# Two-layer hybrid encoder with expert layer on one core: expert weights loaded in half units, twenty slots in place of ten

## The chip, the cores and the metric

The kernel runs on one core of one Trainium2 chip. The time is that of the device, in microseconds (us), from launch to end; the span is from the first to the last instruction in the profile of one execution. Smaller is better.

## The reference

Two layers over 256 tokens of width 1024, all in float32. Each layer has a mixing part (pooling and neighbourhood attention between two projections) and a channel part: a dense SwiGLU in layer 0, and in layer 1 eight expert SwiGLUs of which each token takes two. The last part is what the change touches:

```python
logits = jnp.einsum('td,de->te', xt, w_router)
top_logit, top_idx = lax.top_k(logits, TOP_K)          # TOP_K = 2 of 8 experts
gates = jax.nn.softmax(top_logit, axis=-1)
...
def run_block(args):                                   # tokens of one expert
    tok, gate, e = args
    xb = xt[tok]
    a = xb @ w_gate[e]                                 # 1024 x 3584
    b = xb @ w_up[e]                                   # 1024 x 3584
    y = (jax.nn.silu(a) * b) @ w_down[e]               # 3584 x 1024
    return y * gate[:, None]
```

Each expert has three matrices of 14.7 MB, 352 MB in all, and each is read once.

## The kernel before

The expert layer is done item by item, items 0 to 7, one expert each in the order of their token counts. An item has room for 96 tokens (three groups of 32) or 64 (two groups): `ITEM_CAP` is 96, 64, 96, 96, 64, 96, 96, 64. If counts are larger, a loop at the end runs extra items; these inputs need none.

The weights of an item come as 24 *units* of 3,584 columns by 128 partitions (1,792 KB), into ten slots of SBUF used in a ring: 8 for the gate matrix (one row tile of 128 rows each), 8 for up, and 8 for down, which is laid out so that a partition holds 28 rows of 1,024 in a run, in two halves of 14 rows, and a unit is 3.5 of these rows. `load_unit` on SyncE issues one transfer for a unit and raises `unit_landed[slot]`. Its loop waits before each issue until TensorE has raised `unit_done` for the unit that held the slot. The first ten units are loaded ahead, each as soon as the buffers under its slot are free: mixing buffers of layer 1 lie there.

TensorE runs `expert_item`. For gate and up it takes one unit after the other (`landed` waits for it), and for each of two halves (1,792 columns) and each group s calls `project_tokens`: four matmuls of 32 columns of tokens by 448 columns of weights, which run side by side in the four quarters of the array. `unit_done` rises once a unit, behind both halves. The last unit of each part also raises `gate_done` and `up_done` half by half, and ScalarE (Silu, L1141) and VectorE (product L1454, transpose L1459) turn the banks into `e`, whose `e_ready` the down part waits for. The down part goes through pairs of units: rows 0 to 2 of seven for all groups, then a wait for the second unit, row 3, and rows 4 to 6. After rows 0 to 2 of the second half come `combine` of the item before and `turn_picks`, and after row 3 `gather` for the next item.

The instruction streams are unrolled for items 0 to 7. SyncE's queue carries the unit loads alone in this phase, up to the two output transfers.

Of the kernel before, what the change touches and what calls it, by code (L numbers as in the profile page):

```python
# [12 lines left out]
P = 128  # L13
D = 1024
DT = D // P
# [17 lines left out]
FE = 3584  # L33
# [8 lines left out]
FH = FE // 2  # L42
FJ = FH // 4
DJ = D // 4
FT = FH // P
# [9 lines left out]
DENSE_LOADS = 3 * DBLOCKS  # L55
MOE0 = 2 * MIX_LOADS + DENSE_LOADS
assert 2 * MOE0 % STAGE == 0
UNIT = FE
SLOTS = 10
EXTRA_SLOTS = 8  # L60


def ffn_order(blocks):
# [6 lines left out]

DENSE = ffn_order(DBLOCKS)

UNITS = 3 * DT
EXTRA_TURNS = UNITS // EXTRA_SLOTS
HALF_UNITS = DT // 2
BANKS = 2 * TG
PARTS = BANKS - 1
assert UNITS % EXTRA_SLOTS == 0 and HALF_UNITS * UNIT == FT * D
# [20 lines left out]
def hybrid_encoder(nc, x, mix_pre, mix_post, ffn_pre, ffn_post, w_in, pool_w, pool_scale, rpb,  # L99
                   w_out, d_gate, d_up, d_down, router, e_gate, e_up, e_down, consts, out):  # L100
    with ExitStack() as ctx:
# [76 lines left out]
        e = hid[:, :, :, :].rearrange("p h s (t r) -> p h s t r", r=Q)  # L178
# [175 lines left out]
        MH = 2 * MOE0  # L354

        def quad(j):
            return slice(Q * j, Q * (j + 1))
# [4 lines left out]
        def ready_count(i, half, s, groups):  # L362
            return i * BANKS + (half * TG + (TG if s == groups - 1 else s + 1))
# [10 lines left out]
        def unit_slot(i, u):  # L374
            return (i * UNITS + u) % SLOTS if isinstance(i, int) else u % EXTRA_SLOTS

# [19 lines left out]
        def _(sp):  # L396
# [31 lines left out]
                            load(MIX_LOADS + j, by_tile(w[0])[:, :, cut], DT)  # L428

            def load_unit(i, expert, u):  # L430
                part, v = u // DT, u % DT
                if part == 2:
                    src = e_down[0, expert].rearrange("e (h p t) n -> p (e h) (t n)", h=2, p=P)
                    at = v % HALF_UNITS * UNIT
                    src = src[:, v // HALF_UNITS, at:at + UNIT]
                else:
                    src = (e_gate, e_up)[part][0, expert].rearrange("e (t p) n -> p (e t) n", p=P)[:, v, :]
                slot = unit_slot(i, u)
                sp.dma_start(units[slot][:, :], src).then_inc(unit_landed[slot], 16)

            zeroth = slice(0, 1)
            sp.wait_ge(scored, GROUPS * DEPTH)
            load_unit(0, zeroth, 0)
            sp.wait_ge(delta_dve_ready, DEPTH)
            load_unit(0, zeroth, 1)
            sp.wait_ge(pv_done, GROUPS * DEPTH)
            sp.wait_ge(delta_ready, 3 * DEPTH)
            for u in range(2, 5):
                sp.wait_ge(split_ready, 2 * (MOE0 - 4 + u))
                load_unit(0, zeroth, u)  # L450
            for u in range(5, 9):
                sp.wait_ge(half_done, MH - max(7 - u, 0))
                load_unit(0, zeroth, u)
            sp.wait_ge(rms_post, 2 * 3)
            load_unit(0, zeroth, 9)
            for u in range(SLOTS, UNITS):
                sp.wait_ge(unit_done, u - SLOTS + 1)
                load_unit(0, zeroth, u)
# [192 lines left out]
        def _(pe):  # L651
# [253 lines left out]
            def expert_item(i, groups, before, after, first=False, last=False, extra=False):  # L905

                def landed(u):
                    pe.wait_ge(unit_landed[unit_slot(i, u)], unit_loads(i, u) * 16)

                def project_tokens(dt, u, half, s):  # L910
                    w = units[unit_slot(i, u)]
                    for j in range(4):
                        at = half * FH + j * FJ
                        ins = mm(bank(half, s)[quad(j)], xT[:, s, dt, :], w[:, at:at + FJ],  # L914
                                 start=dt == 0, stop=dt == DT - 1)
                    return ins

                def project_hidden(half, u, tiles, s):
                    for t in tiles:
                        for j in range(4):  # L920
                            at = t * D + j * DJ
                            w = units[unit_slot(i, u + at // UNIT)][:, at % UNIT:at % UNIT + DJ]
                            ins = mm(down_out[s][quad(j)], e[:, half, s, t, :], w, start=half == t == 0 and s != 2,  # L923
                                     stop=half == 1 and t == FT - 1, skip_group_check=s == 2)
                    return ins

                pe.wait_ge(x_ready, i + 1)
                if not first:
                    pe.wait_ge(facc_done, ends(i) if extra else i)
                for dt in range(DT):  # L930
                    landed(dt)
                    for half in range(2):
                        for s in range(groups):
                            ins = project_tokens(dt, dt, half, s)
                            if dt == DT - 1 and (half, s) != (1, groups - 1):
                                ins.then_inc(gate_done, count_step(half, s, groups))
                    ins.then_inc(unit_done, 1)
                for dt in range(DT):
                    u = DT + dt
                    landed(u)  # L940
                    for half in range(2):
                        for s in range(groups):
                            if dt == 0:
                                pe.wait_ge(silu_done, ready_count(i, half, s, groups))
                            ins = project_tokens(dt, u, half, s)
                            if dt == DT - 1 and (half, s) != (1, groups - 1):
                                ins.then_inc(up_done, count_step(half, s, groups))
                    ins.then_inc(unit_done, 1)
                if not first:
                    pe.wait_ge(y_act, i)  # L950
                for v in range(0, DT, 2):
                    half, u = v // HALF_UNITS, 2 * DT + v
                    h0 = 2 * DT + half * HALF_UNITS
                    row = 7 * (v % HALF_UNITS) // 2
                    landed(u)
                    for s in range(groups):
                        if v % HALF_UNITS == 0:
                            pe.wait_ge(e_ready, ready_count(i, half, s, groups))
                        project_hidden(half, h0, range(row, row + 3), s)
                    if v == HALF_UNITS:  # L960
                        if not (first or extra):
                            combine(i - 1, before)
                        turn_picks(i, groups)
                    landed(u + 1)
                    for s in range(groups):
                        ins = project_hidden(half, h0, range(row + 3, row + 4), s)
                    ins.then_inc(unit_done, 1)
                    if v == HALF_UNITS:
                        pe.wait_ge(spread_ready, i + 1)
                        gather(i + 1, after)  # L970
                    for s in range(groups):
                        ins = project_hidden(half, h0, range(row + 4, row + 7), s)
                    ins.then_inc(unit_done, 1)
                if last or extra:
                    combine_end(i, groups)

# [20 lines left out]
        def _(act):  # L997
# [136 lines left out]
            def expert_item(i, groups, first=False, extra=False):  # L1134
                for half in range(2):
                    for s in range(groups):
                        if (half, s) == (1, groups - 1):
                            act.wait_ge(unit_done, i * UNITS + DT)
                        else:
                            act.wait_ge(gate_done, i * PARTS + bank_count(half, s, groups))  # L1140
                        act.activation(hid[:, half, s, :], bank(half, s), ACT.Silu).then_inc(  # L1141
                            silu_done, bank_step(s, groups))
                act.wait_ge(spread_tp, i + 1)
                if not first:
                    act.wait_ge(comb_done, ends(i) - 1 if extra else i)
                act.activation(spread[:, :, 0:groups, :], pa[:, :].rearrange("p (t s n) -> p t s n", t=NT, n=P)[  # L1146
                    :, :, 0:groups, :], ACT.Copy).then_inc(spread_ready, 1)
                act.wait_ge(unit_done, i * UNITS + UNITS)
                both = pd[:, :].rearrange("p (b n) -> p b n", b=2)[:, :, 0:DJ]
                ins = act.activation(y[:, 0:2, :], both, ACT.Copy)  # L1150
                if groups == TG:
                    ins = act.activation(y[:, 2, :], down_out[2], ACT.Copy)
                ins.then_inc(y_act, 1)
# [28 lines left out]
        def _(dve):  # L1182
# [259 lines left out]
            def hidden(i, half, s, groups):  # L1442
# [5 lines left out]
                if order >= 2:  # L1448
                    dve.wait_ge(e_ready, ready_count(i, (order - 2) // groups, (order - 2) % groups, groups))
                if (half, s) == (1, groups - 1):  # L1450
                    dve.wait_ge(unit_done, i * UNITS + 2 * DT)
                else:
                    dve.wait_ge(up_done, i * PARTS + bank_count(half, s, groups))
                dve.tensor_tensor(buf.rearrange("p t r -> p r t"),  # L1454
# [100 lines left out]
```

## Time and profile before

| | |
|---|---|
| median of 3 runs | 1385.05 us (1382.86 to 1386.51) |
| the profiled execution | 1383.68 us |
| its span | 1381.9 us |
| granted TensorE clock, mean | 0.981 of full speed |
| TensorE busy | 1293.9 us, 94% |
| ScalarE, VectorE busy | 278.1 and 421.2 us |
| bytes moved | 443.42 MB, mean 321 GB/s |
| expert phase, from TensorE's first matmul on a unit | 547.5 us to the end |

The span has the two mixing parts and the dense part in its first 540 us, and the expert phase behind. Engines are named as PE (TensorE matmuls), PEld (TensorE weight loads), DVE (VectorE), ACT (ScalarE), POOL (GpSimd) and SPq (SyncE's queue of DMA issues). The time of a busy TensorE is modelled from issue times, so it can read full where it is merely fed in order. The TensorE clock has two levels, 2.4 GHz (1.00) and 1.2 GHz (0.50).

### The profile page before, as it was taken

What the parts mean: (1) busy time and instruction counts of PE and PEld (TensorE: products, weight loads), DVE (VectorE), ACT (ScalarE), POOL (GpSimd) and SP (SyncE); (2) the same over time, 40 slices, a digit from 0 to 9 for tenths busy, and PEclk for the clock granted to TensorE, in tenths of its full rate; (3) what the DMA queues carried; (4) which work ended last, traced back from release to release, by engine and by line L of the source; (5) the groups of instructions that cost most, each with busy time, mean ns of one, the idle gap of its engine ahead of it and who ended that gap; (6) DMA issues with size and microseconds to landing.
All of it is one profiled execution on the core that took longest, in us unless ns stands there. A gap on an engine that the chain in (4) does not pass through costs nothing.

```text
span 1381.9 us, 30957 instructions
## 1 busy us (share of the span) xinstructions
PE 1293.9 (94%) x14359; PEld 803.1 (58%) x14359; DVE 421.2 (30%) x573; ACT 278.1 (20%) x409; POOL 103.7 (8%) x239
## 2 busy tenths in 40 slices
PE   5788999999989886999999999999989999999985
PEld 5776999999978874336344345346334345336333
DVE  5586644444455754011020031030021031031023
ACT  4355444433343533000000000000000000000001
POOL 3231400000000123700000000000000000000000
PEclk9999999999998999999999999999999999999998
DMA  9716755555554057999999999999999999999992
GB/s 312 241 62 215 218 186 185 188 188 187 186 195 148 34 228 320 379 406 389 408 426 424 426 424 424 426 425 425 425 425 426 425 427 422 428 423 424 421 416 97
DMA packets 63734, 443.42 MB, mean 321 GB/s; under 512 B 4440, under 2 KB 6496, under 8 KB 39024
## 3 DMA queue, kind: packets, MB, share of 16 engines
q1 hardware_dynamic: 61456, 433.46, 77.4%
q0 software_dynamic: 2144, 7.90, 2.0%
q8 instruction: 117, 1.92, 0.6%
q14 instruction: 17, 0.14, 0.0%
HBM read 440.30 MB, written 1.05 MB: 319 GB/s over the span
## 4 chain that ended last, share of the span: by engine, by line
PE 83%; DMA 7%; DVE 5%; ACT 1%; SPq 1%; issue 1%; POOL 0%; ACTq 0%; DVEq 0%
PE pd L923 17%; PE pa L914 13%; PE pb L914 13%; PE pc L914 9%; DMA unit<-in_moe_w_down 5%; PE pc L656 3%; PE pc L657 3%; PE pc L658 3%; PE pd L658 2%; PE pd L657 2%; PE pd L656 2%; DMA rwords_b<-in_na_rpb 2%; PE pa L656 2%; PE pa L658 2%; PE pa L657 2%; PE pa L868 2%
## 5 line engine op out<-in xcount | busy, mean ns | idle before, releaser
L923 PE MATMUL pd<-unit,hid 128*32 128x256 f32 x4704 | 260.2, 379 | 9.8 <-DMA unit<-in_moe_w_down 9.8
L914 PE MATMUL pa<-unit,xT 128*32 128x448 f32 x2048 | 240.2, 541 | 3.3 <-DMA unit<-in_moe_w_up 2.1
L914 PE MATMUL pb<-unit,xT 128*32 128x448 f32 x2048 | 240.3, 541 | 0.0
L923 PEld LDWEIGHTS pd<-unit,hid 128*32 128x32 f32 x4704 | 151.2, 110 | 116.4 <-DMA unit<-in_moe_w_down 11.9
L1196 DVE TENSOR_TENSOR w_lo<-ring,w_hi 128x2048 fp32r<-128x2048 f32 x72 | 170.7, 2372 | 139.6 <-ACT w_hi L1012 139.2
L1454 DVE TENSOR_TENSOR hidp<-hid,pa 128x448 f32<-128x448 f32 x16 | 14.8, 924 | 558.4 <-PE pa L914 558.4
L1012 ACT ACTIVATE w_hi<-ring 128x2048 fp32r<-128x2048 f32 x72 | 137.3, 1908 | 69.9 <-PE pb L658 56.4
L914 PE MATMUL pc<-unit,xT 128*32 128x448 f32 x1280 | 149.5, 539 | 0.0
L914 PEld LDWEIGHTS pa<-unit,xT 128*32 128x32 f32 x2048 | 66.3, 110 | 128.1 <-issue 120.4
L914 PEld LDWEIGHTS pb<-unit,xT 128*32 128x32 f32 x2048 | 66.6, 110 | 126.6 <-issue 126.6
L656 PE MATMUL pc<-hT_hi,w_hi 128*128 128x256 f32 x448 | 130.1, 290 | 5.4 <-DVE w_lo L1196 4.0
L657 PE MATMUL pc<-hT_lo,w_hi 128*128 128x256 f32 x448 | 128.7, 287 | 0.0
L658 PE MATMUL pc<-hT_hi,w_lo 128*128 128x256 f32 x448 | 128.5, 287 | 0.0
L1146 ACT ACTIVATE spread<-pa 128x768 f32<-128x768 f32 (+1 forms) x8 | 5.9, 733 | 441.5 <-PE pa L901 441.5
L656 PEld LDWEIGHTS pc<-hT_hi,w_hi 128*128 128x128 f32 x448 | 88.2, 197 | 6.2 <-DVE w_lo L1196 4.1
L657 PEld LDWEIGHTS pc<-hT_lo,w_hi 128*128 128x128 f32 x448 | 88.2, 197 | 0.0
L658 PEld LDWEIGHTS pc<-hT_hi,w_lo 128*128 128x128 f32 x448 | 88.0, 196 | 0.0
L914 PEld LDWEIGHTS pc<-unit,xT 128*32 128x32 f32 x1280 | 41.5, 110 | 78.8 <-issue 78.8
L658 PE MATMUL pd<-hT_hi,w_lo 128*128 128x256 f32 x256 | 72.4, 283 | 0.0
L657 PE MATMUL pd<-hT_lo,w_hi 128*128 128x256 f32 x256 | 72.4, 283 | 0.0
L656 PE MATMUL pd<-hT_hi,w_hi 128*128 128x256 f32 x256 | 72.4, 283 | 0.0
L1141 ACT ACTIVATE hid<-pa 128x448 f32<-128x448 f32 x16 | 8.7, 545 | 229.8 <-PE pa L914 229.3
(261 smaller groups left out, 1321.9 us busy)
## 6 DMA issues: line engine op xcount, KB each, us to landing
unit<-in_moe_w_gate SPq DMA_DIRECT2D x64, 1792.0 KB, 27.7
unit<-in_moe_w_up SPq DMA_DIRECT2D x64, 1792.0 KB, 26.9
unit<-in_moe_w_down SPq DMA_DIRECT2D x64, 1792.0 KB, 28.8
ring<-in_dense_w_gate SPq DMA_DIRECT2D x8, 2048.0 KB, 8.9
ring<-in_dense_w_up SPq DMA_DIRECT2D x8, 2048.0 KB, 8.9
ring<-in_dense_w_down SPq DMA_DIRECT2D x8, 2048.0 KB, 7.6
ring<-in_w_in SPq DMA_DIRECT2D x7, 2048.0 KB, 7.9
ring<-in_w_out SPq DMA_DIRECT2D x4, 2048.0 KB, 11.7
```

Source lines behind the costliest of these rows:

```text
L656: mm(dst, still[0], moving[0], start=start, stop=False)
L657: mm(dst, still[0], moving[1], start=False, stop=False)
L658: return mm(dst, still[1], moving[0], start=False, stop=stop)
L868: ins = mm(gather_out[s][quad(j)], pick[:, t, Q * s:Q * (s + 1)], blocks, start=t == 0, stop=t == NT - 1)
L914: ins = mm(bank(half, s)[quad(j)], xT[:, s, dt, :], w[:, at:at + FJ], start=dt == 0, stop=dt == DT - 1)
L923: ins = mm(down_out[s][quad(j)], e[:, half, s, t, :], w, start=half == t == 0 and s != 2, stop=half == 1 and t == FT - 1, skip_group_check ...
L1012: act.activation(hi, src, ACT.Copy).then_inc(hi_ready, 1)
L1141: act.activation(hid[:, half, s, :], bank(half, s), ACT.Silu).then_inc(silu_done, bank_step(s, groups))
L1146: act.activation(spread[:, :, 0:groups, :], pa[:, :].rearrange("p (t s n) -> p t s n", t=NT, n=P)[:, :, 0:groups, :], ACT.Copy).then_inc(s ...
L1196: dve.tensor_tensor(lo, src, hi.bitcast(F32), ALU.subtract).then_inc(split_ready, 1)
L1454: dve.tensor_tensor(buf.rearrange("p t r -> p r t"), hid[:, half, s, :].rearrange("p (r t) -> p r t", t=FT), bank(half, s).rearrange("p (r ...
```

## The change

A unit becomes half as wide: `UNIT = FH`, 1,792 columns of one gate or up row tile, or 1.75 rows of down weights. There are twenty slots in the same SBUF, 48 units an item, and so twice as many transfers, each of 896 KB with 7,168 bytes in a run for each partition instead of 14,336. The first ten row tiles are loaded in pairs under the waits of before (`load_row`). TensorE waits for and frees each half by itself, except the last row tile of gate and of up, whose two halves are freed together. In the down part the loop over rows is outside and the one over groups inside; a row waits for the units that begin in it, and a unit is freed behind the row in which it ends. The points of `combine`, `turn_picks` and `gather` are the same.

```diff
-UNIT = FE
-SLOTS = 10
-EXTRA_SLOTS = 8
+UNIT = FH
+SLOTS = 20
+EXTRA_SLOTS = 16
-UNITS = 3 * DT
+UNITS = 6 * DT
-HALF_UNITS = DT // 2
+HALF_UNITS = DT
             def load_unit(i, expert, u):
-                part, v = u // DT, u % DT
+                part, v = u // (2 * DT), u % (2 * DT)
...
-                    src = (e_gate, e_up)[part][0, expert].rearrange("e (t p) n -> p (e t) n", p=P)[:, v, :]
+                    src = (e_gate, e_up)[part][0, expert].rearrange("e (t p) n -> p (e t) n", p=P)
+                    src = src[:, v // 2, v % 2 * UNIT:(v % 2 + 1) * UNIT]
...
+            def load_row(k):
+                for u in range(2 * k, 2 * k + 2):
+                    load_unit(0, zeroth, u)
...
                 for dt in range(DT):
-                    landed(dt)
                     for half in range(2):
+                        u = 2 * dt + half
+                        landed(u)
                         for s in range(groups):
-                            ins = project_tokens(dt, dt, half, s)
+                            ins = project_tokens(dt, u, half, s)
...
-                    ins.then_inc(unit_done, 1)
+                        if dt < DT - 1:
+                            ins.then_inc(unit_done, 1)
+                        elif half:
+                            ins.then_inc(unit_done, 2)
...
-                for v in range(0, DT, 2):
-                    half, u = v // HALF_UNITS, 2 * DT + v
-                    h0 = 2 * DT + half * HALF_UNITS
-                    row = 7 * (v % HALF_UNITS) // 2
-                    landed(u)
-                    for s in range(groups):
-                        if v % HALF_UNITS == 0:
-                            pe.wait_ge(e_ready, ready_count(i, half, s, groups))
-                        project_hidden(half, h0, range(row, row + 3), s)
-                    if v == HALF_UNITS:
-                        if not (first or extra):
-                            combine(i - 1, before)
-                        turn_picks(i, groups)
-                    landed(u + 1)
-                    for s in range(groups):
-                        ins = project_hidden(half, h0, range(row + 3, row + 4), s)
-                    ins.then_inc(unit_done, 1)
-                    if v == HALF_UNITS:
-                        pe.wait_ge(spread_ready, i + 1)
-                        gather(i + 1, after)
-                    for s in range(groups):
-                        ins = project_hidden(half, h0, range(row + 4, row + 7), s)
-                    ins.then_inc(unit_done, 1)
+                for half in range(2):
+                    h0 = 4 * DT + half * HALF_UNITS
+                    for t in range(FT):
+                        first_unit, last_unit = t * D // UNIT, ((t + 1) * D - 1) // UNIT
+                        for u in range(first_unit, last_unit + 1):
+                            if u * UNIT >= t * D:
+                                landed(h0 + u)
+                        for s in range(groups):
+                            if t == 0:
+                                pe.wait_ge(e_ready, ready_count(i, half, s, groups))
+                            ins = project_hidden(half, h0, t, s)
+                        if (t + 1) * D % UNIT < D:
+                            ins.then_inc(unit_done, 1)
+                        if half and t == 2:
+                            if not (first or extra):
+                                combine(i - 1, before)
+                            turn_picks(i, groups)
+                        if half and t == 3:
+                            pe.wait_ge(spread_ready, i + 1)
+                            gather(i + 1, after)
```

## Rows read from the trace of the kernel before

**Rows 1.** The page: busy time of the engines, and its 40 slices.
```profile
PE 1293.9 (94%) x14359; PEld 803.1 (58%) x14359; DVE 421.2 (30%) x573; ACT 278.1 (20%) x409; POOL 103.7 (8%) x239
...
DMA  9716755555554057999999999999999999999992
```

**Rows 2.** Stretches of the expert phase: from:to, length, busy us, clock, DMA share, GB/s.
```profile
547.00:619.90 72.90, 72.39 (x772) 25.12 (x776) 4.00 (x7) 3.27 (x6) 30.80 (x143) 1.00 0.90 363
706.90:737.30 30.40, 30.40 (x554) 18.69 (x548) 8.86 (x20) 0.60 (x1) 0.00 (x0) 1.00 1.01 426
737.30:809.40 72.10, 72.10 (x772) 24.96 (x768) 3.49 (x5) 3.87 (x7) 0.00 (x0) 1.00 1.01 425
809.40:851.20 41.80, 41.80 (x766) 25.47 (x758) 10.86 (x22) 0.81 (x1) 0.00 (x0) 1.00 1.01 425
965.10:1013.00 47.90, 47.90 (x512) 16.27 (x504) 1.89 (x3) 3.05 (x6) 0.00 (x0) 1.00 1.01 426
1013.00:1032.10 19.10, 13.09 (x230) 7.18 (x227) 5.42 (x13) 0.00 (x0) 0.00 (x0) 1.00 1.00 422
1326.40:1347.10 20.70, 16.90 (x252) 8.05 (x244) 7.27 (x15) 0.00 (x0) 0.00 (x0) 0.92 0.97 411
1347.10:1365.60 18.50, 18.41 (x324) 11.41 (x324) 3.59 (x7) 0.60 (x1) 0.00 (x0) 1.00 0.30 124
```

**Rows 3.** TensorE's timeline in item 7: start, length, instructions, idle before and its releaser.
```profile
1338.55 2.80 PE L923 MATMUL pd<-unit,hid 128*32 128x256 f32 x48 [0.63 <-DMA unit<-in_moe_w_down]
1342.84 3.66 PE L923 MATMUL pd<-unit,hid 128*32 128x256 f32 x64 [1.49 <-DMA unit<-in_moe_w_down]
1347.13 2.80 PE L923 MATMUL pd<-unit,hid 128*32 128x256 f32 x48 [0.63 <-DMA unit<-in_moe_w_down]
```

**Rows 4.** DMA from 700 to 1300 us: packets by size; queue, packets, MB, share.
```profile
DMA packets 19984, 254.84 MB, mean 425 GB/s; under 512 B 2215, under 2 KB 2215, under 8 KB 2215
...
q1 hardware_dynamic: 19916, 253.77, 100.0%
```

**Rows 5.** The chain that ended last, its end: start, length, what.
```profile
1311.41 35.68 DMA unit<-in_moe_w_down
1347.13 2.80 PE pd L923 x48
...
1356.91 8.68 PE pd L923 x160
```

**Rows 6.** Timeline of TensorE and SyncE's queue around the first refill.
```profile
547.51 0.96 PE L914 MATMUL pa<-unit,xT 128*32 128x448 f32 x8 [1.25 <-DVE xT L1422]
...
549.03 0.94 PE L914 MATMUL pc<-unit,xT 128*32 128x448 f32 x8
...
552.28 22.88 SPq L439 DMA_DIRECT2D unit<-in_moe_w_up  x6
```

**Rows 7.** The unit loads (L439) issued from 552 to 560 us.
```profile
DMA to landing us min/median/max: 7.2/8.0/8.8
```

**Rows 8.** The unit loads (L439) issued from 640 to 662 us.
```profile
L439 SPq DMA_DIRECT2D unit<-in_moe_w_up x3: 332/332/333, 655.0 to 661.9; - x3
...
DMA to landing us min/median/max: 8.7/9.4/11.0
```

**Rows 9.** DMA from 153.4 to 155.4 us, packets of 2 KB: packets, MB, share.
```profile
q1 hardware_dynamic: 400, 0.82, 105.0%
```

**Rows 10.** DMA from 437.4 to 439.4 us, packets of 4 KB.
```profile
q1 hardware_dynamic: 206, 0.84, 102.4%
```

**Rows 11.** Timeline at the start of item 0's down part.
```profile
619.34 0.91 DVE L1454 TENSOR_TENSOR hidp<-hid,pc 128x448 f32<-128x448 f32 x1
619.69 2.56 PE L923 MATMUL pd<-unit,hid 128*32 128x256 f32 x44
...
620.28 0.65 DVE L1459 STREAM_TRANSPOSE hid<-hidp 128x448 f32<-128x448 f32 x1
```

**Rows 12.** DMA from 1340 to 1370 us in 40 slices of 0.75 us.
```profile
DMA  9999999664544635446444331200000000000000
GB/s 440 421 401 459 421 440 421 268 287 194 229 191 191 268 153 248 210 191 268 175 210 191 134 134 57 90 0 0 0 0 0 0 0 0 0 0 0 0 22 0
```

More of the change, by code:

```diff
@@ L441, in _ @@
             zeroth = slice(0, 1)
+            def load_row(k):
+                for u in range(2 * k, 2 * k + 2):
+                    load_unit(0, zeroth, u)
             sp.wait_ge(scored, GROUPS * DEPTH)
-            load_unit(0, zeroth, 0)
+            load_row(0)
             sp.wait_ge(delta_dve_ready, DEPTH)
-            load_unit(0, zeroth, 1)
+            load_row(1)
             sp.wait_ge(pv_done, GROUPS * DEPTH)
             sp.wait_ge(delta_ready, 3 * DEPTH)
[L448 to L453, printed above, removed]
+            for k in range(2, 5):
+                sp.wait_ge(split_ready, 2 * (MOE0 - 4 + k))
+                load_row(k)
+            for k in range(5, 9):
+                sp.wait_ge(half_done, MH - max(7 - k, 0))
+                load_row(k)
             sp.wait_ge(rms_post, 2 * 3)
-            load_unit(0, zeroth, 9)
+            load_row(9)
             for u in range(SLOTS, UNITS):
@@ L912, in project_tokens @@
                     for j in range(4):
-                        at = half * FH + j * FJ
+                        at = j * FJ
                         ins = mm(bank(half, s)[quad(j)], xT[:, s, dt, :], w[:, at:at + FJ],
@@ L916, in project_tokens, with project_hidden @@
                     return ins
[L918 to L924, printed above, removed]
+                def project_hidden(half, u, t, s):
+                    for j in range(4):
+                        at = t * D + j * DJ
+                        w = units[unit_slot(i, u + at // UNIT)][:, at % UNIT:at % UNIT + DJ]
+                        ins = mm(down_out[s][quad(j)], e[:, half, s, t, :], w, start=half == t == 0 and s != 2,
+                                 stop=half == 1 and t == FT - 1, skip_group_check=s == 2)
                     return ins
@@ L930, in expert_item @@
                 for dt in range(DT):
-                    landed(dt)
                     for half in range(2):
+                        u = 2 * dt + half
+                        landed(u)
                         for s in range(groups):
-                            ins = project_tokens(dt, dt, half, s)
+                            ins = project_tokens(dt, u, half, s)
                             if dt == DT - 1 and (half, s) != (1, groups - 1):
                                 ins.then_inc(gate_done, count_step(half, s, groups))
-                    ins.then_inc(unit_done, 1)
+                        if dt < DT - 1:
+                            ins.then_inc(unit_done, 1)
+                        elif half:
+                            ins.then_inc(unit_done, 2)
                 for dt in range(DT):
-                    u = DT + dt
-                    landed(u)
                     for half in range(2):
+                        u = 2 * DT + 2 * dt + half
+                        landed(u)
                         for s in range(groups):
@@ L947, in expert_item @@
                                 ins.then_inc(up_done, count_step(half, s, groups))
-                    ins.then_inc(unit_done, 1)
+                        if dt < DT - 1:
+                            ins.then_inc(unit_done, 1)
+                        elif half:
+                            ins.then_inc(unit_done, 2)
                 if not first:
                     pe.wait_ge(y_act, i)
-                for v in range(0, DT, 2):
-                    half, u = v // HALF_UNITS, 2 * DT + v
-                    h0 = 2 * DT + half * HALF_UNITS
-                    row = 7 * (v % HALF_UNITS) // 2
-                    landed(u)
-                    for s in range(groups):
-                        if v % HALF_UNITS == 0:
-                            pe.wait_ge(e_ready, ready_count(i, half, s, groups))
-                        project_hidden(half, h0, range(row, row + 3), s)
-                    if v == HALF_UNITS:
-                        if not (first or extra):
-                            combine(i - 1, before)
-                        turn_picks(i, groups)
-                    landed(u + 1)
-                    for s in range(groups):
-                        ins = project_hidden(half, h0, range(row + 3, row + 4), s)
-                    ins.then_inc(unit_done, 1)
-                    if v == HALF_UNITS:
-                        pe.wait_ge(spread_ready, i + 1)
-                        gather(i + 1, after)
-                    for s in range(groups):
-                        ins = project_hidden(half, h0, range(row + 4, row + 7), s)
-                    ins.then_inc(unit_done, 1)
@@ new lines, in expert_item @@
+                for half in range(2):
[10 more added lines that the diff above has]
+                        if (t + 1) * D % UNIT < D:
+                            ins.then_inc(unit_done, 1)
+                        if half and t == 2:
[5 more added lines that the diff above has]
+                            gather(i + 1, after)
@@ L1137, in expert_item @@
                         if (half, s) == (1, groups - 1):
-                            act.wait_ge(unit_done, i * UNITS + DT)
+                            act.wait_ge(unit_done, i * UNITS + 2 * DT)
                         else:
@@ L1450, in hidden @@
                 if (half, s) == (1, groups - 1):
-                    dve.wait_ge(unit_done, i * UNITS + 2 * DT)
+                    dve.wait_ge(unit_done, i * UNITS + 4 * DT)
                 else:
```

## Prediction

> **What bounds the kernel now.** I read the page first, for where the time is. In its slices the expert phase is more than half the span, and there both TensorE and the DMA engines read nine tenths or more [rows 1]. Two full engines do not say which one is late, so the second view is the stretches of the phase. An item with 96 slots costs TensorE 72.1 us for its 16 gate and up units, 4.51 us a unit, and 41.8 us for the 8 down units with combine and gather; an item with 64 slots costs 47.9 us (3.0 us a unit) and 30.4 us [rows 2]. So TensorE wants 113.9 us or 78.3 us for an item. The transfers take the same time for each. How long is in the third view, TensorE where it waits: in item 7, the last, it starts again at 1338.55, 1342.84 and 1347.13 us, each time released by a unit that landed, 4.29 us apart [rows 3]. Twenty-four units are then 103 us: DMA is faster than a long item, and 25 us slower than a short one. Over the five long and three short items TensorE wants 804 us, and transfers at 4.29 us for 192 units 824 us. From 706.9 us to 1300 us the DMA share never reads under 1.00 [rows 2, 4], while TensorE waits a few us in the last two thirds of two short items (13.09 us busy of 19.10, 16.90 of 20.70) [rows 2]. So what ends last is the queue of transfers: it never runs dry after the first item, it decides when the item 7's unit 20 (the fifth down unit) lands, and only 18.5 us of TensorE work and the final norm lie behind that [rows 2, 5]. The chain says the same: 35.68 us of transfer up to 1347.13 us, then only TensorE [rows 5]. A cost on each byte's transfer is paid in full. TensorE's own time is paid only behind the last wait.
>
> In item 0 it is otherwise. The first refill waits until TensorE has finished unit 0: issued at 552.28 us, with TensorE started at 547.51 us [rows 6]. It lands in 7.2 us [rows 7], of which 4.29 us are pace and 2.9 us latency. From there slots come free every 4.51 us, slower than 4.29 us, so the queue is shallow: at 640 to 662 us a unit still lands 8.7 us after its issue, 1.5 us more than with an empty queue [rows 8]. Behind that, short item 1 frees slots every 3.0 us and the queue stays deep to the end.
>
> **The transfers, cut in two.** Bytes, order and engines stay. A unit is now one packet of 14,336 bytes for each of 128 partitions: 8 packets on each of 16 DMA engines, and one small completion word. (17,700 large packets and 2,215 small ones in 600 us are this 8 to 1 [rows 4].) After the change it is 16 packets of 7,168 bytes and two words. No row shows a 7,168-byte packet, so I take its pace from packets of other sizes, in stretches of 2 us where nothing else moves and all engines are full. 2 KB: 400 packets, so 16 x 2 us / 400 = 80.0 ns [rows 9]. 4 KB: 206 packets, 155.3 ns [rows 10]. The line through them is 4.7 ns a packet and 0.0368 ns a byte. It gives 531.8 ns at 14,336 bytes; the measured 4,290 / 8 = 536 ns are 4.4 ns more, with the completion word in them. So the line holds over a sevenfold size. At 7,168 bytes it gives 268.3 ns. Sixteen are 4,292 ns against 8 x 531.8 = 4,254 ns: 38 ns more for two half units. The second completion word I price like any packet, 5 ns. The pace becomes 4.29 + 0.043 = 4.333 us for the bytes of one unit, 1.0% slower.
>
> Bounds: a packet constant and a word that cost nothing give 4.290 us. From above: the shares in the same rows count 105.0% and 102.4% busy, so a packet is held for 84.0 and 159.1 ns, and that line has a constant of 8.9 ns; if none of this overlapped, eight more packets and a word are 80 ns, 4.370 us. I take 4.333 us, as the packet counts are throughput and the shares are occupancy.
>
> How many units pay: the wait that decides is for the item 7's unit 20. From the first refill (unit 10 of the phase) to there are 178 units: 178 x 0.043 = +7.6 us (bounds 0 and +14.2 us).
>
> A rule of the Trainium skill bears on that constant. By "DMA: Bandwidth & Descriptors", section "Why small descriptors are slow (HBM only)", each packet pays a fixed overhead of some 3 cycles; with the 850 MHz of the same page's "Where 436 GB/s comes from" that is 3.5 ns, an estimate from the page, below the 4.7 ns of [rows 9, 10]. Eight more packets would then be 28 ns a unit and 178 units +5.0 us, where the rows give +7.6 us.
>
> **The start of the refilling.** The slot of half unit 0 comes free after 2.26 us of TensorE work instead of 4.51 us, so the first refill goes out at about 550.0 us, 2.26 us earlier. Of such a lead only what the queue holds can survive the shallow stretch, and that was 1.5 us at its thinnest [rows 8]: -1.5 us for every later landing. Together +6.1 us for the second half of the deciding unit.
>
> **The finer wait.** Before, TensorE starts rows 0 to 2 of that second down half when all of unit 20 is there, and needs 2.80 us (0.87 us a row, from 160 instructions, ten rows, in 8.68 us [rows 5]). After, row 0 starts on the first half unit, 2.17 us sooner, and rows 1 and 2 (1.74 us) remain behind the second. The combine therefore comes 6.1 - 0.9 = 5.2 us later. Nothing behind it is late again: the last half unit is wanted by row 12, which starts about 14 us behind the combine's start, and it lands three units or 13.0 us behind the second half of unit 20, so 11.3 us behind the combine's start.
>
> **Edits that cost nothing where they lie.** Twice as many issues: 0.33 us each on SyncE's queue [rows 8], 384 of them against 2.17 us of transfer each; behind them on that queue stand only the next loads and the output. Twice the landing waits on TensorE: a boundary shows no gap, since six steps of 0.75 us [rows 6] are already the 4.51 us of a unit. Down rows looped over t outside and groups inside: the same matmuls and weight loads, but groups 1 and 2 of row 0 are wanted sooner. In item 0 the down part starts at 619.69 us, group 2's row 0 would be due 0.86 us later at 620.55 us, and its transpose ends at 620.93 us [rows 11]: 0.4 us in a long item. In a short one, with group 1 wanted 0.43 us into the part and not 1.3 us, at most 0.9 us. Sum 5 x 0.4 + 3 x 0.9 = 4.7 us if it all counted; the queued transfers hide it: already at 662 us a unit lands up to 11.0 us after its issue, 3.8 us more than with an empty queue [rows 7, 8], the depth grows from there, and in items 4 and 7 TensorE waits for transfers anyway. The gate and up parts' last bank frees both half units at once, as before. The nine prefetched units land 9 x 0.04 = 0.4 us later, and the last of them isn't wanted until 588 us.
>
> **Sum:** +7.6 - 1.5 - 0.9 = +5.2 us on the profiled execution's 1383.7 us, so 1388.9 us. Its span is 1381.9 us; the 1.8 us around it stay. The runs' median is 1385.05 us, 1.4 us above the profiled one, which gives 1390.2 us, 0.37% slower. A measurement of this kernel can tell about 0.3%, or 4.2 us, from no change, and the forecast lies just beyond that.
>
> **Rivals.**
> - *The packets are cheap.* The constant is under 4 ns at this size, or the 4.4 ns above the line shrink with shorter packets. For it: it is so small that a count of 205 and not 206 in [rows 10] would move it, and a single ns decides. Against it: two sizes far below 7 KB, and the line's hit at 14 KB. With half of it, 2.4 ns for each of eight packets and the word, 178 units cost +3.8 us and the sum is +1.4 us (1386.5 us); with no cost at all it is -2.4 us (1382.7 us). Both are within 0.3%. Chance 0.33. By the Trainium skill's 3 cycles (the section above) the sum would be +5.0 - 2.4 = +2.6 us, an estimate from that page, 1387.7 us and within 0.3% too; the line from the two sizes speaks against it, by 1.2 ns.
> - *The packets are dear.* Each packet start also repeats some of the 4.4 ns, or nothing overlaps: up to +14.2 - 1.5 - 0.9 = +11.8 us, 1396.9 us. For it: the occupancy of [rows 9, 10]. Against it: occupancy isn't pace. Chance 0.12.
> - *Faster.* The wait ends with the slowest DMA engine. From about 1345 us the engines' share drops to a half and stays there for some 11 us [rows 12]: half the engines are done that much sooner. If finer transfers made the slow ones lose less (each stop would end with 7 KB in front of it and not 14 KB), at most that lag, about 11 us, would come back. It decides from a gain of 9.4 us, which turns +5.2 us into -4.2 us. Nothing shows that the lag hangs on the unit. Chance 0.05.
> - *TensorE's new waits.* The 4.7 us of transposes reach the path, because an item that waited for transfers now waits for both. In the last item that is 0.9 us on top of +5.2 us at worst; with all of it, 1394.9 us. Chance 0.04.
>
> The forecast as it stands, a constant of 4 to 6 ns, has 0.46, with a range of its own from 1389.0 to 1392.3 us (nine times 4 or 6 ns on 178 units, less 2.4 us). The range for 8 in 10 is 1384.0 to 1396.0 us: it leaves out the free packet and the dearest ones. Faster 0.05. Slower 0.46 x 0.9 (its lower edge lies within 0.3%) + 0.12 + 0.04 = 0.57. Same is the rest, 0.38.
>
> **What would show it.** DMA packets rise by 24,576 large and 3,072 small to 91,382. In a stretch of full transfers the rate falls from 425 GB/s to about 421 GB/s, and TensorE's waiting starts in the last item come in steps of 2.17 us, not 2.145 us. The first refill is issued near 550.0 us and lands in about 5.1 us. The start of the rows behind the last combine comes 5 us later. The prediction is wrong if the rate stays at 425 GB/s (cheap), falls under 419 GB/s (dear), or if the last rows of TensorE wait for something other than a unit.

## The result, and the profile after

The changed kernel takes 1388.43 us (median of 16 runs, 1385.66 to 1392.38); the kernel before, over all its runs beside it, 1382.49 us (16 runs, 1375.14 to 1386.51). The ratio is 1.006, 95% interval 1.0044 to 1.0077, so it is 0.6% slower, clear of noise. The forecast was 1390.2 us, from a base of 1385.05 us: +5.2 us, where the medians now differ by 5.9 us and the ratio makes it some 8 us. Ratios here and below leave out disturbed executions; in e2_packets that is one of seven, of 1882.95 us at a granted clock of 0.67.

The page after, its slices and its packets. The busy times and the digits look like those of [rows 1]; what differs is the rate under them and the number of packets.

```profile
PE 1295.7 (94%) x14359; PEld 798.4 (58%) x14359; DVE 419.9 (30%) x573; ACT 277.9 (20%) x409; POOL 103.0 (7%) x239
...
DMA  9616755555554068999999999999999999999993
...
DMA packets 91384, 443.44 MB, mean 320 GB/s; under 512 B 7512, under 2 KB 9568, under 8 KB 91248
```

DMA from 700 to 1300 us, against [rows 4]. The same 600 us move 249.71 MB and not 253.77 MB, though the queue is busy all the time. The mean of 418 GB/s lies under the 419 GB/s that the prediction had named as the sign of dear packets.

```profile
DMA packets 39259, 250.80 MB, mean 418 GB/s; under 512 B 4355, under 2 KB 4355, under 8 KB 39189
...
q1 hardware_dynamic: 39189, 249.71, 100.8%
```

The timeline of TensorE in item 7, ahead of the last combine, against [rows 3]. The starts after a landing are now 2.18 us apart on average (8.71 us for four from 1345.10 us on), which is 4.355 us for the bytes of a whole unit, against 4.29 us.

```profile
1345.10 1.93 PE L927 MATMUL pd<-unit,hid 128*32 128x256 f32 x32 [1.10 <-DMA unit<-in_moe_w_down]
1347.29 1.93 PE L927 MATMUL pd<-unit,hid 128*32 128x256 f32 x32 [0.26 <-DMA unit<-in_moe_w_down]
...
1353.81 1.93 PE L927 MATMUL pd<-unit,hid 128*32 128x256 f32 x32 [1.06 <-DMA unit<-in_moe_w_down]
```

The end of the chain, against [rows 5]. It still runs through a transfer of down weights until TensorE may do rows 1 and 2 of the second half; only then come the combine and the last ten rows.

```profile
1328.94 24.83 DMA unit<-in_moe_w_down
1353.81 1.93 PE pd L927 x32
...
1362.73 8.68 PE pd L927 x160
```

The first refill, against [rows 6]: TensorE's first expert matmul, then SyncE's issue 2.52 us behind it, where it had been 4.77 us. It lands in 4.8 us.

```profile
545.31 0.96 PE L919 MATMUL pa<-unit,xT 128*32 128x448 f32 x8 [1.24 <-DVE xT L1430]
```
```profile
547.83 25.13 SPq L440 DMA_DIRECT2D unit<-in_moe_w_up  x12
```

The transfers issued from 640 to 662 us, against [rows 8]: the soonest lands in 5.3 us where it was 8.7 us, the median in 7.2 us where it was 9.4 us. Each carries half the bytes, which is some 2.2 us less by itself, so this alone doesn't show an earlier queue.

```profile
DMA to landing us min/median/max: 5.3/7.2/10.2
```

**A yardstick inside the profile.** Here the first expert matmul comes at 545.31 us and before at 547.51 us, though nothing ahead of it was changed except loads that nobody waits for; in a second profile of the kernel before it comes at 541.70 us. Single executions differ by that much ahead of the expert phase. So I compare the stretch from TensorE's first expert matmul to the start of its last ten rows: 1356.73 - 547.51 = 809.2 us before and 1362.54 - 545.31 = 817.2 us after, +8.0 us.

A sharper yardstick for the pace alone lies between two like waits. In items 4 and 7, both short, TensorE waits for the fifth down unit (after the change, for its second half). Between the two waits 72 units land. The item 4 waits of before and after, from their chains, stand below; those of item 7 are at 1347.13 us [rows 5] and 1353.81 us (above).

```profile
1032.09 2.80 PE pd L923 x48
```
```profile
1033.59 1.93 PE pd L927 x32
```

That is 315.04 us before and 320.22 us after, 4.376 and 4.447 us a unit; the second profiles of both kernels (e10_before, e11_after below) give 315.00 and 320.20 us.

### The profile page after: what moved, and what is told of

Read it like the earlier page. It is cut to its first block, busy times and chain, and to the rows that moved or that the text cites. A ratio compares the mean times of both kernels' runs of the same rounds, so it can differ in the third digit from the quotient of the medians.

```text
span 1384.6 us, 31423 instructions
## 1 busy us (share of the span) xinstructions
PE 1295.7 (94%) x14359; PEld 798.4 (58%) x14359; DVE 419.9 (30%) x573; ACT 277.9 (20%) x409; POOL 103.0 (7%) x239
## 4 chain that ended last, share of the span: by engine, by line
PE 81%; DMA 7%; DVE 7%; ACT 1%; issue 1%; SPq 1%; POOL 0%; ACTq 0%; DVEq 0%
PE pd L927 16%; PE pa L919 13%; PE pb L919 12%; PE pc L919 8%; DMA unit<-in_moe_w_down 4%; PE pc L661 3%; PE pc L662 3%; PE pc L663 3%; PE pd L663 2%; PE pd L662 2%; PE pd L661 2%; DMA rwords_b<-in_na_rpb 2%; DMA unit<-in_moe_w_up 2%; PE pa L663 2%; PE pa L661 2%; PE pa L662 2%
## 5 line engine op out<-in xcount | busy, mean ns | idle before, releaser
L927 PE MATMUL pd<-unit,hid 128*32 128x256 f32 x4704 | 263.4, 380 | 12.6 <-DMA unit<-in_moe_w_down 9.5
```

## The experiments

Ratios are against runs of the kernel before on the same chip, with 95% intervals; "stretch" is the first yardstick above, "72 units" the second.

| run | packets | ratio | stretch, us | 72 units, us | MB in 700 to 1300 us |
|---|---|---|---|---|---|
| before | 14,336 B | 1 | 809.2 | 315.0 | 253.77 |
| after | 7,168 B | 1.006 (1.0044 to 1.0077) | 817.2 | 320.2 | 249.71 |
| e1_whole | 14,336 B | 0.9986 (0.9966 to 1.0006) | 810.2 | 316.8 | 253.56 |
| e2_packets | 7,168 B | 1.0061 (1.0039 to 1.0082) | 820.0 | 319.6 | 250.34 |
| e4_quarter | 3,584 and 7,168 B | 1.0167 (1.0145 to 1.0188) | 831.8 | 325.8 | 245.12 |
| e7_parity | 14,336 B, twice the transfers | 1.0015 (0.9995 to 1.0034) | 809.2 | 315.1 | 253.75 |
| e5_hybrid | 14,336 B, halves at two places | 0.9979 (0.9959 to 0.9999) | 806.7 | - | 253.64 |
| e6_big | as e5, part 28,672 B | 0.9971 (0.9954 to 0.9987) | 804.6 | - | 253.87 |

In the last two TensorE no longer shows a wait for that unit in item 7.

### Whole transfers under the new waits (e1_whole)

```diff
 (the changed kernel; landing counted once for a pair of half units)
-                    src = src[:, v // 2, v % 2 * UNIT:(v % 2 + 1) * UNIT]
+                    src = src[:, v // 2, :]
...
-                sp.dma_start(units[slot][:, :], src).then_inc(unit_landed[slot], 16)
+                sp.dma_start(pairs[pair][:, :], src).then_inc(unit_landed[pair], 16)
```

> The changed kernel with its half-unit waits, releases and row order on TensorE, but each pair of half units is again one transfer with packets of 14,336 bytes. Packet theory (the slower pace of the 7,168-byte packets is the whole loss): the pace returns to 4.29 us for a unit's bytes, the rate from 700 to 1300 us to 425 GB/s, and the time to that of the kernel before, within 2 us. Rival, TensorE's new waits in the row order reach the path: 3 to 6 us slower than before, at 425 GB/s.

Measured: median 1378.41 us of 12 runs, ratio 0.9986. The loss goes away when only the half transfers are taken back. Everything on TensorE's side (twice the releases, the row order, the earlier wish for the transposed groups) stayed in and costs nothing that the time shows. So the rival with TensorE's waits falls. Whether packets or the number of transfers cost is left to the next two. In this profile the deciding unit came 5.97 us behind the one before it (1340.23 to 1346.20 us) and not 4.29 us; without that one late landing the stretch would read 808.5 us.

### Small packets alone (e2_packets)

```diff
 (the kernel before; a slot is two chunks with 32 bytes behind each)
+            return units[slot][:, 0:parts * (n + PAD)].rearrange("p (a n) -> p a n", a=parts)[:, :, 0:n]
...
-                sp.dma_start(units[slot][:, :], src).then_inc(unit_landed[slot], 16)
...
+                src = src.rearrange("p (a n) -> p a n", a=parts)
+                sp.dma_start(chunks(slot, parts), src).then_inc(unit_landed[slot], 16)
```

The ahead-loaded unit 6 also waits for one more half of the mixing part, since the gaps move its end.

> The kernel before, with whole units, ten slots and one transfer a unit, but each slot has a gap of 32 bytes in its middle, so that a transfer consists of 7,168-byte packets. Packet theory: 8 more packets per engine and unit at 8 ns each, pace 4.36 us a unit, rate 418 to 419 GB/s, and with neither the earlier start nor the finer wait the time is 10 to 13 us above before. Rival, the number of transfers and completion words costs and not the packets: same as before within 2 us.

Measured: median 1391.78 us of 7 runs, ratio 1.0061, stretch +10.8 us. One transfer and one completion word for each unit as before, and the whole loss is there. DMA from 700 to 1300 us of this run:

```profile
DMA packets 37174, 251.40 MB, mean 419 GB/s; under 512 B 2183, under 2 KB 2183, under 8 KB 37107
...
q1 hardware_dynamic: 37107, 250.34, 100.7%
```

The 2,183 completion words are the count of before (2,215), at the rate of after. In the time, 0.61% is 8.4 us (5.4 to 11.3), a little under the 10 to 13 us expected; the stretch lies inside. The 72 units take 4.5 us more, which is 7.8 ns for each of the eight added packets.

### Twice the transfers alone (e3_transfers, e7_parity)

```diff
 (the kernel before, landing counted to 32; e3: two runs of 64 neighbouring partitions)
-                sp.dma_start(units[slot][:, :], src).then_inc(unit_landed[slot], 16)
+                for k in range(0, P, P // 2):
+                    sp.dma_start(units[slot][k:k + P // 2, :], src[k:k + P // 2]).then_inc(unit_landed[slot], 16)
 (e7: even and odd partitions)
+                for k in range(2):
+                    sp.dma_start(units[slot][k::2, :], src[k::2]).then_inc(unit_landed[slot], 16)
```

> The kernel before, but each unit comes as two transfers of 64 partitions each, with packets of 14,336 bytes: as many transfers and completion words as in the changed kernel, and no more data packets than before. Packet theory: one more completion word of 5 ns a unit, at most 1 us in all, same as before within 2 us, 424 to 425 GB/s. Rival, the number of transfers: 10 to 13 us slower, 418 GB/s.

Measured: median 2126.95 us of 6 runs, which scatter from 1906.99 to 2130.93 us. Neither theory had this. The profiled execution is one of the longest, 2130.93 us. The experiment changed two things: each transfer covered only half of the partitions, and neighbouring ones. In the profile, DMA from 1000 to 1200 us shows the engines busy all the time at half the rate:

```profile
DMA packets 3829, 43.96 MB, mean 220 GB/s; under 512 B 764, under 2 KB 764, under 8 KB 764
...
q1 hardware_dynamic: 3816, 43.76, 100.3%
```

3,816 - 764 = 3,052 large packets in 200 us on 16 engines are 1,049 ns each instead of 536 ns. So this run says nothing on the number of transfers, and I made it again with partitions that spread.

> The kernel before, but each unit comes as two transfers, one of the even and one of the odd partitions, with packets of 14,336 bytes. Packet theory: as many data packets as before and one more completion word, some 10 ns a unit, 2 us in all, 424 GB/s. Rival, the number of transfers is what costs: 10 us or more slower, 418 GB/s. If the rate falls far below 400 GB/s, as with 64 neighbouring partitions, the partitions that one transfer covers decide it, and the run says nothing on either.

Measured: median 1382.69 us, ratio 1.0015, and the rate of before with twice the completion words:

```profile
DMA packets 22194, 254.82 MB, mean 425 GB/s; under 512 B 4426, under 2 KB 4426, under 8 KB 4426
...
q1 hardware_dynamic: 22125, 253.75, 100.1%
```

The number of transfers is not the cost of 8 us. The time puts it at 2 us, with zero inside the interval and 4.7 us at its upper end (0.34%); the profile puts it at less, since the stretch is the 809.2 us of before and the 72 units take 315.1 us against 315.0 us.

### The dose (e4_quarter)

```diff
 (e2_packets with four chunks for gate and up units, two for down; the slot's gaps to match)
-                slot, parts = unit_slot(i, u), 2 if part == 2 else 2
+                slot, parts = unit_slot(i, u), 2 if part == 2 else 4
```

> As the kernel before with 7,168-byte packets in the down units, and packets of 3,584 bytes in the gate and up units (gaps of 32 bytes in a slot). If every packet start costs its 4.7 ns of the line and also repeats the 3.7 ns of stall that the changed kernel shows, 24 more packets are 202 ns a gate or up unit and 8 more are 67 ns a down unit, 157 ns on average: 178 units give 28 us more, rate near 411 GB/s. If only the 4.7 ns of the line repeat: 88 ns on average, 16 us more. If the halving costs by something else than the number of packets, 10 to 13 us as in the run with 7,168-byte packets.

Measured: median 1404.71 us, ratio 1.0167, which is 23 us (20 to 26), and stretch +22.6 us, between the 16 us and the 28 us expected and above the 10 to 13 us of the third case. It moved 245.12 MB in the 600 us:

```profile
DMA packets 58425, 246.16 MB, mean 410 GB/s; under 512 B 2134, under 2 KB 2134, under 8 KB 58359
...
q1 hardware_dynamic: 58359, 245.12, 101.3%
```

A unit is 1.835 MB, so 600 us give 4.339 us a unit before, 4.398 us in e2 and 4.492 us here. Divided by the packets that an engine does more (8 in e2; 24, 24 and 8, on average 18.7, here), that is 7.4 ns and 8.2 ns a packet; by the 72 units it is 7.8 and 8.0 ns. The price is close to constant for each packet, and it is nearer to the full 8.4 ns (4.7 ns and the 3.7 ns more) than to the 4.7 ns of the line. In the changed kernel the same reckoning gives 4.409 us: 70 ns for eight packets and one completion word. The time grew by less than 178 x 0.153 = 27 us would say. What is missing lies ahead of item 4's wait: up to there e4 is about 12 us longer, where 106 units at 0.150 us would be 16 us. That fits refills in item 0, where slots come free only every 4.51 us, hiding part of the price. But in e2 nothing is missing (+10.8 us, where 178 x 0.063 is 11.2 us), so it stays open.

### What the finer transfers give back (e5_hybrid, e8_lead, e9_tail)

```diff
 (the changed kernel; load_unit issues n half units at once)
+            if 20 <= i * UNITS + u < 68 or (i, u // 2) == (NE - 1, 5 * DT // 2):
+                return 1
...
+            return 2
```

> As the changed kernel, but with whole transfers (packets of 14,336 bytes) everywhere except the refills behind the first twenty half units up to the fifth row tile of item 1's up... that is half units 20 to 67 of the phase, and the two half units whose landing is waited for ahead of the last combine. If the earlier start is worth 1.5 us and the finer last wait 0.9 us, as the sum had it, the time is 1 to 4 us below before (-0.1 to -0.3%); the first refill is issued 2.3 us after TensorE's first unit, and the rate from 700 to 1300 us is 425 GB/s. If neither is worth anything the time is that of the run with whole transfers everywhere, within 1 us.

Measured: 1377.85 us, ratio 0.9979, stretch 806.7 us, 2.5 us under before. The direction and the size are those expected, and the interval just leaves out 1. Then each place alone, with a second profile of both kernels for the yardstick's own spread (one execution each):

> The hybrid without its finer last wait: half transfers only for half units 20 to 67. Measured inside the profile, from TensorE's first expert matmul to the start of its last ten rows (809.2 us before, 810.2 us with whole transfers everywhere, 806.7 us in the hybrid): if the earlier start is worth 1.5 to 2.3 us, 808 to 808.7 us; if the finer wait did all, 810 us.

> The hybrid without its earlier start: half transfers only for the two half units whose landing is waited for ahead of the last combine. From 810.2 us the finer wait gives 809.3 us; if it did all that the hybrid gains, 806.7 us.

> The kernel before, unchanged, to see how far the same stretch of the profile (809.2 us) repeats: if within 1 us, differences of 2 us between single profiles mean something.

> The changed kernel again, for the same: 817.2 us in its first profile, 8.0 us more than before. The packet theory wants 7 to 9 us more in this one as well.

Measured stretches: e8_lead 807.2 us, e9_tail 808.9 us, e10_before 808.2 us, e11_after 817.5 us. The yardstick repeats within 1.0 us for before and 0.3 us for after, so the changed kernel is 8.0 to 9.2 us longer in every pairing. Against e1_whole (810.2 us) the earlier start alone gives 3.0 us, more than the 1.5 to 2.3 us expected, the finer wait alone 1.3 us, both together 3.5 us. But e1_whole has the one late landing of 1.7 us just there, so it is a poor base. Parts of the stretch tell the two gains apart more sharply:

- *The start*: from TensorE's first expert matmul to item 4's wait it is 483.6 to 485.1 us in the five profiles with whole transfers in item 0 (before, e1, e7, e9, e10), and 482.5 and 482.9 us in e8 and e5. The means differ by 1.6 us, with a spread of 1.5 us. This is what is left of the gain, since in e8 and e5 the 24 units that go out as halves also have the small packets.
- *The finer wait*: from item 7's wait for the fourth down unit to the last ten rows it is 13.9 us in before, e8 and e10 and 13.1 us in e5 and e9. That is 0.8 us each time.

### Packets of 28,672 bytes (e6_big)

```diff
+            if i in (1, 2, 3, 5, 6) and u >= 4 * DT:
+                return 4
```

> As the hybrid, and the down weights of items 1, 2, 3, 5 and 6 in transfers of four half units, packets of 28,672 bytes. If the packet cost of 8.4 ns holds on to larger packets, four packets fewer for a unit's bytes and half a completion word are 36 to 40 ns, 40 units give 1.5 us back: 0 to 2 us below the hybrid. If the packet cost ends at 14 KB, the same as the hybrid or a little above it, since slots come free and units land four at a time.

Measured: 1377.99 us, ratio 0.9971, stretch 804.6 us, 2.1 us under the hybrid. The times of the two can't be told apart (0.9979 and 0.9971), the stretch leans to a packet cost that goes on at larger sizes. So does a part of it that repeats well: from item 4's wait to that for the fourth down unit of item 7 it is 310.7 to 310.8 us in five profiles with 14 KB packets (before, e10, e5, e8, e9) and 310.2 us here. Sixteen units lie in it with the larger packets, so each gives back about 30 ns, near the 36 to 40 ns expected. This version is clearly faster than the kernel before, by 0.29% (0.13 to 0.46%), and so faster than both.

## Why the prediction was right, and where a term was off

**What bounds the kernel** was right: the queue of transfers. In e2 and e4 TensorE's work is that of before, and the time follows the pace of the transfers.

**The pace of the half transfers** had the right mechanism and too small a size. It is the term that was off. I took +0.043 us for a unit's bytes. The rows after give +0.070 us by rate (4.339 to 4.409 us), +0.065 us by the starts in item 7 (4.29 to 4.355 us) and +0.072 us by the 72 units. By the prediction's own sign (a rate under 419 GB/s) the packets are dear, which I had given a chance of 0.12, though far from the dearest case of 80 ns. The step from the line to the full queue was wrong: I took the line's 4.7 ns for the whole price of a packet, and what lay above it at 14 KB for a share of time that would not repeat with more packets. The dose run shows that about 3 ns more do repeat. I had also read what lay above the line too low. The 4.29 us are steps between single landings; the 253.77 MB of [rows 4] are 4.339 us a unit, or 542 ns a packet, 10 ns above the line and not 4.4 ns. So "the line holds over a sevenfold size" was too strong. The term is 178 x 0.065 to 0.072 = +11.6 to +12.8 us in place of +7.6 us, if all 178 units pay; e4 suggests that some in item 0 may not. By the Trainium skill's 3 cycles a packet, in "DMA: Bandwidth & Descriptors", "Why small descriptors are slow (HBM only)", it would have been +5.0 us; the runs give more, 7.4 to 8.2 ns a packet where that estimate is 3.5 ns.

**The earlier start** was expected at -1.5 us, as the thinnest queue would hold. The profiles up to item 4's wait give 1.6 us with a spread of 1.5 us, net of the small packets of the first 24 refilled units. If those units pay 0.07 us each, the start itself is worth some 3 us. The sign is right; the size may have been low.

**The finer wait**, -0.9 us: 0.8 us in e5 and e9. The last row of TensorE waited for no unit, as the sum had it.

**The sum** goes by e8: the earlier start with its 24 units is -1.6 us, the other 154 units pay 0.065 to 0.072 us each, +10.0 to +11.1 us, and the finer wait gives -0.8 us. That is +7.6 to +8.7 us, against +8.0 and +9.2 us in the stretch. My +5.2 us was low by the pace term, partly offset by the start.

**Luck in the number.** The forecast of 1390.2 us lies 1.8 us from the measured 1388.43 us because two errors offset: the difference was some 3 us too small, and the base of three runs was 2.6 us above the median of sixteen.

**The edits priced at nothing.** TensorE's earlier wish for the transposes is real: in item 2's down part row 0 starts at 808.37 us with groups 0 and 1 (16 matmuls), and group 2 follows only at 809.67 us.

```profile
808.37 1.05 PE L927 MATMUL pd<-unit,hid 128*32 128x256 f32 x16
...
808.97 0.65 DVE L1467 STREAM_TRANSPOSE hid<-hidp 128x448 f32<-128x448 f32 x1
...
809.67 2.58 PE L927 MATMUL pd<-unit,hid 128*32 128x256 f32 x44 [0.26 <-DVE hid L1467]
```

Group 2's transpose ends at 808.97 + 0.65 = 809.62 us. The chain of the changed kernel even names such steps in the long items. But the transfers had the time, and e1_whole, which has the same waits, is not slower. This rival stays off the path. The number of transfers and SyncE's issues cost 2 us by the time of e7_parity, with zero inside its interval, and nothing by its stretch.

**Faster** stayed at what its chance said. The lag of the slow DMA engines did not shrink: from 1352 us on, half of the engines are idle for some 14 us here too, against the 11 us or so of [rows 12]. DMA from 1345 to 1375 us in 40 slices:

```profile
DMA  9999999997555555555455454554000000000001
GB/s 440 421 392 430 440 412 392 433 411 315 220 229 249 249 229 220 239 220 229 182 213 210 201 210 201 210 231 184 19 0 0 0 0 0 0 0 0 22 0 22
```

**Left open:** what the 3 ns or so beyond the line are. They go with the number of packets between 3.6 and 14 KB, but the 2 KB and 4 KB stretches of [rows 9, 10] are the best 2 us of short loads and may simply not contain them. The lag of half the engines was not taken apart either, nor the single late landings like that in e1_whole.

## What to carry to other kernels

When a kernel ends on a full queue of loads, the bytes in a run count and the number of transfers hardly does: here each packet cost about 8 ns of an engine's time, so 1.4% of the pace when runs went from 14 to 7 KB and 3.5% with mostly 3.5 KB. Make transfers small only where something waits for them, at the first refill of an empty queue and at the last landing, and keep the runs long everywhere else. Take such a constant from a long saturated stretch: the best two microseconds of other loads gave 4.7 ns. And to weigh a microsecond, compare the time between two like waits of one profile, which repeated within 0.1 us, but for one late landing, where whole executions scatter by 10 us.

## What the runs showed of the hardware that was not expected

Two transfers of 64 neighbouring partitions in place of one of 128 halved the rate in the profiled execution: 220 GB/s and 1,049 ns a packet of 14,336 bytes, against 425 GB/s and 536 ns, with 16 engines counted busy in both. As even and odd partitions, two transfers run at 425 GB/s. The quickest of e3's six runs took 1906.99 us, too short for 220 GB/s all along (the 334 MB behind the first ten units would need some 1,520 us at it, and the expert phase starts some 540 us in), so the loss can be smaller; no profile shows that. The Trainium skill's "DMA: Bandwidth & Descriptors", section "The descriptor swizzle", has partitions 0 to 63 on the even ports and 64 to 127 on the odd ones. By that, a transfer of either half reaches eight of sixteen ports. The halved rate agrees with it; no run here shows the ports themselves.
